# Hybrid decoder layer with expert retrieval: retrieval spread over 96 slots, dense stages keyed later, 44 dense tiles instead of 40

## The reference

```python
q = einsum('bsd,dq->bsq', h, w_q).reshape(b, s, 8, 2, 128)      # 8 heads, 2 halves
s1, s2 = q[..., 0, :] @ keys1, q[..., 1, :] @ keys2             # 128 scores each
v1, i1 = top_k(s1, 16);  v2, i2 = top_k(s2, 16)
cand = v1[:, None] + v2[None, :]                                # 256 candidates
best, pos = top_k(cand, 16)
expert_idx = i1[...] * 128 + i2[...]                            # one of 16384
gates = softmax(best)
act = gelu(u_tab[expert_idx] . h)                               # 16 experts, 8 heads
y = sum(gates * act * v_tab[expert_idx])
```

## Time and profile before

| | |
|---|---|
| median of 3 runs | 1755.9 us (1754.61 to 1756.68) |
| profiled execution, its own time | 1757.74 us |
| its span | 1756.0 us |
| PE busy | 1476.3 us (84%) |
| DVE busy | 1204.6 us (69%) |
| ACT busy | 543.5 us (31%) |
| POOL busy | 703.4 us (40%) |
| moved by the DMA engines | 624.46 MB, mean 356 GB/s |

### The profile page before, as it was taken

One profiled execution on the slowest core, in us unless ns is written; L12 is line 12 of the kernel. 1 busy time (PEld: TensorE's weight loads), 2 busy tenths in 40 slices (PEclk: granted clock), 3 DMA queues, 4 the chain that ended last, 5 costly groups with the idle time before them and its releaser, 6 DMA issues.

```text
span 1756.0 us, 20157 instructions
## 1 busy us (share of the span) xinstructions
PE 1476.3 (84%) x7320; PEld 977.8 (56%) x7320; DVE 1204.6 (69%) x2134; ACT 543.5 (31%) x1589; POOL 703.4 (40%) x626
## 2 busy tenths in 40 slices
PE   2979999989999998898899757756699898988865
PEld 1648987878788875666676434424343333333321
DVE  5877886889889988898454477768644545454462
ACT  3003432764311256343210146436411010110132
POOL 1001011000122344555666567556643555454461
PEclk9979999999999999999999966767799999999888
DMA  9999997849969679999999999998999999999996
GB/s 337 386 386 406 403 376 305 308 175 369 356 225 359 233 302 372 379 372 391 358 406 375 357 372 394 343 377 325 376 356 392 359 402 395 352 415 412 406 353 257
DMA packets 149806, 624.46 MB, mean 356 GB/s; under 512 B 33994, under 2 KB 38272, under 8 KB 86528
## 3 DMA queue, kind: packets, MB, share of 16 engines
q0 software_dynamic: 82976, 427.52, 62.4%
q1 hardware_dynamic: 66732, 195.67, 29.1%
HBM read 797.54 MB, written 2.10 MB: 455 GB/s over the span
## 4 chain that ended last, share of the span: by engine, by line
PE 39%; DMA 23%; DVE 22%; issue 6%; POOL 6%; ACT 3%; DVEq 1%; SPq 1%; POOLq 0%; ACTq 0%
DMA u_rows<-in_peer_u,expert 12%; DVE u_rows L2030 10%; PE ps L1216 8%; PE ps L1164 7%; DMA v_rows<-in_peer_v,expert_rows 7%; PE ps L457 5%; PE ps L1066 5%; PE ps L909 4%; POOL v_rows L800 4%; DVE first_acc L486 3%; PE ps L903 2%; PE ps L1131 2%; DMA ada_first<-in_w_ada 2%; DMA dense_rows<-in_dense_v 1%; DVEq L1950 1%
## 5 line engine op out<-in xcount | busy, mean ns | idle before, releaser
L2030 DVE SCALAR_TENSOR_TENSOR u_rows<-u_rows,h 128x1024 f32<-128x1024 f32 (+1 forms) x416 | 593.5, 1467 | 379.9 <-DMA u_rows<-in_peer_u,expert 365.4
L800 POOL DMA_INDIRECT u_rows<-in_peer_u,expert x256 | 333.8, 1304 | 348.0 <-DVE u_rows L2030 265.8
L800 POOL DMA_INDIRECT v_rows<-in_peer_v,expert_rows x210 | 278.5, 1326 | 193.5 <-PE ps L1164 140.1
L1164 PE MATMUL ps<-v_rows,diag 128*32 128x512 f32 x1680 | 266.8, 704 | 84.9 <-DMA v_rows<-in_peer_v,expert_rows 75.8
L1216 PE MATMUL ps<-dense_rows,dense_weight 128*128 128x512 f32 x640 | 286.5, 605 | 13.7 <-DVE dense_sums L2109 6.6
L457 PE MATMUL ps<-h2T,dense_rows 128*128 128x256 f32 x1280 | 284.2, 383 | 3.8 <-ACT dense_weight L1562 3.8
L457 PEld LDWEIGHTS ps<-h2T,dense_rows 128*128 128x128 f32 x1280 | 243.5, 191 | 52.3 <-issue 16.1
L1216 PEld LDWEIGHTS ps<-dense_rows,dense_weight 128*128 128x128 f32 x640 | 121.7, 193 | 178.1 <-issue 169.0
L1164 PEld LDWEIGHTS ps<-v_rows,diag 128*32 128x32 f32 x1680 | 68.1, 126 | 229.8 <-issue 229.4
L308 POOL DMA_DIRECT2D ada_late<-in_w_ada x61 | 32.3, 530 | 304.4 <-DVE ada_acc L322 262.5
L322 DVE SCALAR_TENSOR_TENSOR ada_acc<-ada_late,cact,ada_acc 128x2048 f32<-128x2048 f32 x57 | 133.8, 2348 | 17.1 <-DMA ada_late<-in_w_ada 15.9
(11 more groups left out here) (308 smaller groups left out, 1842.8 us busy)
## 6 DMA issues: line engine op xcount, KB each, us to landing
ada_late<-in_w_ada POOLq DMA_DIRECT2D x61, 1024.0 KB, 7.8
dense_rows<-in_dense_u SPq DMA_DIRECT2D x40, 1024.0 KB, 18.3
dense_rows<-in_dense_v SPq DMA_DIRECT2D x40, 1024.0 KB
ada_first<-in_w_ada SPq DMA_DIRECT2D x64, 512.0 KB, 11.7
ring<-in_w_in SPq DMA_DIRECT2D x10, 2048.0 KB, 24.7
ring<-in_w_o SPq DMA_DIRECT2D x8, 2048.0 KB, 15.0
ring<-in_w_peer_q SPq DMA_DIRECT2D x8, 2048.0 KB, 14.7
opened<-in_w_in SPq DMA_DIRECT2D x8, 1024.0 KB, 13.0
```

The lines of the kernel that those rows point to most:

```text
L800: nc.gpsimd.indirect_dma_start(buf[:, :], None, table, bass.IndirectOffsetOnAxis(ap=places, axis=0), bounds_check=last_sparse, oob_is_err= ...
L1164: ins = nc.tensor.matmul(ps[rows, k, :], diag[n % len(diag)][:, :], v_slot(n)[0][:, 512 * k:512 * k + 512], start=first, stop=last)
L2030: ins = nc.vector.scalar_tensor_tensor(out=u_rows[b][:, lo:hi], in0=u_rows[b][:, lo:hi], scalar=1.0, in1=h2[:, q // H, lo:hi], op0=ALU.mul ...
```

## The change

The change has four parts. The number of dense tiles goes from 40 to 44 (the third buffer of `dense_weight` grows from 4 to 8 tiles). To make room in SBUF, the one-hots are made for 4 tokens at a time instead of 8, in 64 batches instead of 32. The retrieval jobs 1 to 15 are spread over slots 0 to 95 instead of 0 to 66, job 1 over 12 slots and job 2 over 15. The dense tiles of `u`, the first gathers of `v` and the early groups of `v` get later keys, and the spare buffers open at slot 68 instead of 76.

```diff
-DENSE = 40
+DENSE = 44
-BATCH = 8
+BATCH = 4
...
-    dense_weight = [at("dense_weight0", B + 16 * KB, [P, 28, T]), at("dense_weight1", C + 16 * KB, [P, 8, T]), at("dense_weight2", B + 12 * KB, [P, 4, T])]
-    WEIGHT_TILES = 0, 28, 36, 40
+    dense_weight = [at("dense_weight0", B + 16 * KB, [P, 28, T]), at("dense_weight1", C + 16 * KB, [P, 8, T]), at("dense_weight2", B + 8 * KB, [P, 8, T])]
+    WEIGHT_TILES = 0, 28, 36, 44
...
-    LEAD, LAG = 31, 20
+    LEAD, LAG = 39, 20
-    SPARE = [(76, 124), (76, 124), (76, 116), (76, TAIL)]
+    SPARE = [(68, 124), (68, 124), (68, 116), (68, TAIL)]
...
         if n < 2:
-            return 24
+            return 27
         if n < len(v_rows):
-            return 31
+            return 33
...
     def tile_key(i):
-        return 22 + 2 * i
+        return 31 + 17 * i // 10
     def batch_key(i):
-        return HOT_KEY + 9 * i // 5 + (3 if i >= BATCHES else 0)
+        return HOT_KEY + 9 * i // 10 + (3 if i >= BATCHES else 0)
     def piece_key(j):
-        return 166 + 21 * j // 10
+        return 167 + 19 * j // 10
     def retrieval_slots(q):
-        return (5 * q - 5, 5) if q < H else (5 * H - 5 + 4 * (q - H), 4)
+        first = (0, 0, 12, *(27 + 16 * k // 3 for k in range(QJOBS - 2)))
+        return first[q], first[q + 1] - first[q]
```

More of the change, by code:

```diff
@@ L159, in build @@
     tail_rows = dense_rows[2:] + [at("tail_rows", B + 32 * KB, [P, D])]
-    dense_weight = [at("dense_weight0", B + 16 * KB, [P, 28, T]), at("dense_weight1", C + 16 * KB, [P, 8, T]), at("dense_weight2", B + 12 * KB, [P, 4, T])]
-    WEIGHT_TILES = 0, 28, 36, 40
-    low_hot = [at(f"low_hot{b}", B + 4 * b * KB, [P, BATCH, NK]) for b in range(2)]
-    high_hot = [at(f"high_hot{b}", B + 8 * KB + 1280 * b, [P, BATCH, DENSE]) for b in range(2)]
-    slot_rows = at("slot_rows", B + 8 * KB + 2560, [P, 3, P])
+    dense_weight = [at("dense_weight0", B + 16 * KB, [P, 28, T]), at("dense_weight1", C + 16 * KB, [P, 8, T]), at("dense_weight2", B + 8 * KB, [P, 8, T])]
+    WEIGHT_TILES = 0, 28, 36, 44
+    low_hot = [at(f"low_hot{b}", B + 2 * b * KB, [P, BATCH, NK]) for b in range(2)]
+    high_hot = [at(f"high_hot{b}", B + 4 * KB + 704 * b, [P, BATCH, DENSE]) for b in range(2)]
+    slot_rows = at("slot_rows", B + 4 * KB + 1408, [P, 3, P])
     dense_sums = at("dense_sums", B, [P, TT, 512])
@@ L1226, in _ @@
                     tile_scores(i)
-                if n == G2_KEY:
-                    pe.wait_ge(experts_ready, QJOBS)
-                    spread_row("g2b", modc, G2)
                 if n == piece_key(DENSE - 1) + 6:
@@ L1237, in _ @@
                     scattered(i)
+                if n == G2_KEY:
+                    pe.wait_ge(experts_ready, QJOBS)
+                    spread_row("g2b", modc, G2)
                 for j in due(piece_key, DENSE, n):
@@ L1529, in _ @@
                     gelu(0)
[L1530 to L1534, removed]
             def spread_weights(q):
@@ L1590, in _ @@
                 for q in range(1, QJOBS):
-                    if n == sum(retrieval_slots(q)) and q >= 6:
+                    if n == sum(retrieval_slots(q)) and q > 1:
                         exponent(q)
```

## The result

The changed kernel takes 1786.42 us (median; 1783.32 to 1788.39), the kernel before 1755.26 us in the same session. The ratio is 1.0175 [1.0154, 1.0196], +31 us, against a forecast of 1756 us and a range of 1735 to 1774 us. The profiled execution after has a span of 1784.4 us, 28.4 us more.

The account below looks back on a forecast made before the run. The mixer was taken as bound by transfers, with PE close behind in two stages. Landmark 0.5, later bytes -5.4, one-hots +2 and pieces +3 summed to 0 us, giving 1756 us, range 1735 to 1774 us.

Parts of the forecast that it names:

- I take 17: Dense u stage: 17 us of waits, from a possible 0 to 40, atop PE's 357.6 us, ending S43 at 996 us.
- both waits: Dense u stage: PE's waits for v rows and for dense loads into two buffers (2.6 us per three-tile run) shrink to half.
- the second rival: PE bounds the dense u stage: all waits stay, S43 at 1014 to 1019 us, total 1776 us; chance 0.20.
- The landmark: End of the last dense u tile, POOL waiting at slot 103: moves 0 to +1 us, from -16 to +23.
- I charge +2 us: Start of dense u tiles: S2 at about 621 us against 618.71 before, after slot 27 at 598 and an exponent at 617.
- The 28 us won early and most of the saved bytes are used up before the landmark: Early dots run some 28 us ahead, but transfers idle while PE works until the last dense u tile ends.
- Bytes: Whole kernel: net -9.4 MB at 383 GB/s, worth 24.6 us wherever transfers are the limit.
- the -5.4 us behind the landmark: After the last dense u tile: 273.6 MB instead of 275.6 MB at the same pace, giving -5.4 us.
- The largest rival, transfers alone: Transfers decide everywhere and the tiles' PE work hides: -24.6 us, 1731 us, or 1743 us with half; chance 0.30.
- One-hots: One-hot stage: batches of four add 27 us of DVE work, mostly covered by idle time; +2 us taken, 0 to 27.
- pieces: From 1283 us: four more dense pieces of v add 28 us to PE, fitting narrowly; +3 us, from 0 to +14.
- The signs named ahead: Profile after: S2 near 621 us, S43 near 996, dense_rows waits 1 to 3 us, DMA share below 0.95 before S43's end.

Follow-up runs that it names:

- e2: The changed kernel with each dense u score summed over 14 of its 16 parts, all loads kept: 1786.03 us, ratio 1.0183.
- e9: e5 with each dense u score summed over 14 of its 16 parts, all loads kept: 1775.74 us, ratio 1.0126.
- e13: e9 with the dense u loads also cut to those 14 parts, 5.8 MB less: 1761.17 us, ratio 1.0047.
- e5: The changed kernel with the spare buffers taking v rows from slot 84, not 68: 1772.44 us, ratio 1.0094.
- e11: The kernel before (40 tiles) with the spare buffers taking v rows from slot 72, not 76: 1762.51 us, ratio 1.0045.
- e14: The kernel before with only the changed kernel's spread retrieval and the exponents that go with it: 1738.28 us, ratio 0.9922.
- e18: e14 with the change's later groups of v (LEAD 39 for 31, spare buffers from slot 68, not 76): 1737.71 us, ratio 0.9911.
- e1: The changed kernel's schedule with 40 dense tiles and one-hots for 8 tokens: 1757.35 us, ratio 1.0018.
- e7: The kernel before with gathers skipping the rows of 44 tiles instead of 40, 17.8 MB less: 1727.21 us, ratio 0.9848.
- e8: The changed kernel with gathers skipping only the rows of 40 tiles, 17.8 MB more: 1809.99 us, ratio 1.0307.
- e3: The kernel before with one-hots for 4 tokens in 64 batches, gate row behind them, pieces one slot later: 1759.95 us, ratio 1.0026.
- e6: The changed kernel with one of each v piece's eight products left out, loads kept: 1778.3 us, ratio 1.0121.
- e10: e5 with one of each v piece's eight products left out, loads kept: 1763.99 us, ratio 1.0047.
- e15: e1 with ACT taking the first six dense tiles out earlier, ahead of the exponent: 1762.54 us, ratio 1.006.
- e16: e5 with ACT taking the first six dense tiles out earlier, ahead of the exponent: 1783.11 us, ratio 1.0178.

## Why the prediction was wrong

**The step that failed** is "I take 17" for what comes on top of PE's 357.6 us of work between S2 and the end of S43. It measured 29: S2 started at 626.0 us and S43 ended at 1012.8. With S2 5 us late that is the whole of 996 against 1013 us. Of the 29 us, PE waited 22.4 (600 to 1014 us: total us, times, longest; 12.5 of the first row lie ahead of S2):

```profile
PE ps L457 <- ACT dense_weight L1558: 15.1, 2, 12.5
PE ps L457 <- DMA dense_rows<-in_dense_u: 12.7, 6, 2.7
PE ps L1165 <- DMA v_rows<-in_peer_v,expert_rows: 7.0, 2, 4.0
```

I had let both waits shrink to half. That for `v` rows shrank by more (39.1 us before), that for dense tiles stayed near its bound of 6 x 2.6 = 15.6 us. The other 6.8 us I had put at nothing: PE was busy for 364.4 us, not 357.6.

```profile
626.00:1012.80 386.80, 364.41 (x1888) 274.99 (x1889) 272.96 (x620) 125.32 (x465) 172.55 (x131) 0.98 0.87 334
```

After three of the six waits for dense rows a tile took 8.8 us (7.17 without), at a granted clock of 0.80 to 0.81, a mean between its two levels:

```profile
738.87 8.81 PE L457 MATMUL ps<-h2T,dense_rows 128*128 128x256 f32 x32 [2.50 <-DMA dense_rows<-in_dense_u]
```

The place is near the one that the second rival named (S43 at 1014 to 1019 us, decisive "from about 25 us of waits on"). Its mechanism was only half right: the tile's *work* was not the bound, since an eighth less of it won nothing, with the stall (e2) or without (e9). What PE waits for is dense tiles and `v` rows that arrive late, and shorter dense loads did help (e13).

**The landmark.** I wrote that POOL waits for the last tile at slot 103 in both kernels, and priced it at 15.61 us as before. The mechanism was right and the size wrong: the wait there grew from 4.30 to 30.9 us, and it stops not only the `v` rows but every `u` row behind it in the same queue. e5 sizes it at 14 us of the 31, e11 at 8 us in a kernel that had none of the rest. I had used S43's end as a date to be reached, and not asked what else stands in that queue if it is late. In e5 S43 ends only 1.7 us earlier and slot 104 comes 26 us earlier.

**S2: "I charge +2 us".** It was 7.3 us later than before, not 2.3, since slot 27 came at 605.1 us, not 598, and the exponent at 623.78, not 617. Between slots 12 and 27 DVE waited 9.2 us for `u` rows, and my sum for these slots had no such wait. But the price of beginning the tiles late is not S2's date. e14, e18 and e1 put the later dates of tiles and first gathers at 17 to 19 us, and the numbers that go with it are PE's busy time up to 673 us and POOL's wait for the groups. I wrote: "The 28 us won early and most of the saved bytes are used up before the landmark". With the tiles left where they were, 14 us of it reach the end.

**Bytes.** One rate for all bytes was wrong. Skipped rows gave 1.3 to 1.5 us per MB (e7, e8), dense loads took about 2.4 (e13). For the change that is an estimate of -25 + 20, about -5 us over the whole kernel, not -24.6; the -5.4 us behind the landmark don't show. The largest rival, transfers alone, had a share of 0.97 in its favour. In the dense `u` stage that share did not price a byte: there skipped rows gave some 0.5 to 1.5 us per MB (e8, e7), where 385 GB/s makes 2.6.

**One-hots and pieces.** +4.6 us for the one-hots, within 0 to 27 and near the +2 taken (e3, and the stage itself). From slot 104 to 168 DVE was busy for 217.62 us instead of 200.82, 17 us more of the 27 that I had worked out for all batches, and the cover mostly held: DVE's wait for `u` rows behind the burst of slot 104 was 24.6 us (1036 to 1304 us), 47.2 in the earlier trace rows. The pieces: +7.4 us behind slot 168, of which about 6 by e6 and e10, within 0 to +14. Together the stages make 16.4 + 4.6 + 7.4 = 28.4 us, against 0.5 - 5.4 + 2 + 3.

**The signs named ahead** mostly worked. PE's waits for `dense_rows` in runs of three were 1.35 to 2.71 us, as the ring of two gives; the DMA share was 0.92, under 0.95; S43 lay past 1005 us. S2's start was a poor sign: it was 5 us late, and e15, where S2 doesn't wait at all, is no faster than e1.

**What stays open.** That the tiles' keys alone cost the 17 to 19 us (the first gathers moved with them), how the late tiles come to hold up POOL's gathers of `v`, where e13's second half lies, and why e16 is 15 us slower than e5.

## What to carry to other kernels

A DMA share of 0.97 doesn't say what a byte is worth in that stage: take bytes away from one kind of transfer and see at which landmark the time comes. Where one queue issues the gathers for two consumers, price a late buffer by everything that stands behind it in the queue, and move the gather that needs it rather than the work it waits for. Begin the large work as soon as it can begin if its engine is idle early and nearly full later, and look at whose buffers it holds when it is late: in e1 PE caught up, but POOL stood 44 us longer. Change one date at a time, since here a good edit (14 us) was hidden under one that cost more.

## What the runs showed of the hardware

A row that a gather skips by its bound moves next to no data, as I wrote of the kernel before, but it is not free: it leaves a packet under 512 B. Between the kernel before and e7 the queue keeps its 82976 packets while the bytes fall from 427.52 to 409.72 MB; only the packets under 512 B grow, from 33994 to 36169 (the page of e7):

```profile
DMA packets 149807, 606.66 MB, mean 352 GB/s; under 512 B 36169, under 2 KB 40447, under 8 KB 88703
...
q0 software_dynamic: 82976, 409.72, 61.2%
```

The queue's busy time falls from 62.4% of 1756.0 to 61.2% of 1724.2 us, by 41 us, where 17.8 MB at 385 GB/s are 46; the kernel gets 27 of them. The granted clock over the span was 0.90 to 0.93 in all of these kernels. It was 0.921 in the changed kernel and 0.911 before, so it doesn't explain that the changed one is slower.
